# Second attention: the mask goes from a matmul into the running sums on GpSimd, and the query blocks run from last to first

## The chip, the cores and the metric

One Trainium2 chip, one core of it. The metric is the device time of one execution in microseconds (us); lower is better. The kernel before took 2061.19 us in the median of three runs (2055.81, 2061.19 and 2062.60). The profile is of one more execution, which took 2057.08 us.

## The reference, cut to what matters

Two transformer blocks run one after the other on 512 positions of width 1024. The change lies in the attention of the second block ("forgetting attention", 16 heads of 64):

```python
log_f = jax.nn.log_sigmoid(f_logit + b_f)
cum = jnp.cumsum(log_f, axis=1).transpose(0, 2, 1)
for i in range(S // Q_BLOCK):                      # 4 query blocks of 128
    lo, hi = i * Q_BLOCK, (i + 1) * Q_BLOCK
    s = jnp.einsum('bhqd,bhkd->bhqk', q[:, :, lo:hi], k[:, :, :hi]) * scale
    s = s + cum[:, :, lo:hi, None] - cum[:, :, None, :hi]
    s = jnp.where(kpos[None, :] <= qpos[:, None], s, -1e30)
    prob = jax.nn.softmax(s, axis=-1)
    outs.append(jnp.einsum('bhqk,bhkd->bhqd', prob, v[:, :, :hi]))
```

The term `cum[lo:hi]` is constant along a row and drops out of the softmax. Query block i sees 128 x (i + 1) keys, and only its last 128 keys need the mask.

## The kernel before, in words

Each engine has its own program, a list of instructions in a fixed order. Semaphores order them between engines; on an engine nothing overtakes anything. The five programs are `tensor_program` (TensorE, PE), `scalar_program` (ScalarE, ACT), `vector_program` (VectorE, DVE), `pool_program` (GpSimd, POOL) and `sync_program` (SyncE, SP, which issues the weight loads).

Nearly all of the work is dense matmuls of 1024-wide weights. Each product is made of three matmuls of split operands (high times high, low times high, high times low), 24 matmuls of 128 x 512 per weight tile, all on line L719. ACT and DVE split every weight tile into high and low parts (L1259, L1737); SP loads the next tile when a buffer is free.

The second attention runs inside such a stretch. `mix2_order` writes the order out by hand. There are 20 weight tiles (`MIX2`), so 480 dense matmuls. There are 64 score blocks, numbered n. The pair of heads is c = n // 8, the head of the pair is p = n % 2, and the query block is i = n % 8 // 2. Each score block is a step, and step n is followed by a number of slots from the table `share`, by n % 8. The table sums to 32 for each pair of heads. With three more steps at the end this makes 267 slots, and `woven` spreads the 480 dense matmuls evenly over the slots. In step n TensorE issues the transposes of block n - 2 ("turn"), then the scores of block n. In every fourth step (n % 4 == 2) it first issues the value products of blocks n - 5 and n - 3.

A score block goes through the engines in this way:

- TensorE, `fox_scores` (L1128): two matmuls, queries by keys (L918) and queries by the low part of the keys (L921), both 128 x 128(i + 1), into bank 4 or 5. Then a third matmul, identity by `mask_b` in bf16 (L1135), adds 1e30 above the diagonal of the last 128 columns (queries and keys carry the sign so that the smallest score is the largest weight). It first waits until the block two back has been read from that bank (`s_fmin`).
- VectorE, `fox_scores` (L2211): one custom instruction (L2219) adds the row of running sums `at_c` to the scores, writes `at_p`, and takes the row's minimum.
- ScalarE, `fox_scores` (L1609): the exponential with the row sum (L1613).
- VectorE, `fox_divide` (L2222): reciprocal (L2226) and scaling (L2228).
- TensorE, `fox_turn` (L1140): transposes of 128 x 128 (L1146), copied out by ScalarE (L1620). `fox_values` (L1150) multiplies with the values (L1160).

`at_c` has four buffers, one for each head modulo 4, of 128 partitions x 512 sums, all partitions alike. GpSimd loads them from memory (`load_cum`, L2424): heads 0 to 3 at once, head h only when the last block of head h - 4 has been read by L2219. During the stretch these 12 loads are all that GpSimd does.

VectorE and ScalarE also take the dense tiles out of the banks (queries L1930, keys L1942 and L1949, and copies) and split weights. `mix2_scalar_order` and `mix2_vector_order` put these pieces behind the scores and behind the divide of a block, one or two for each block, by the length of the list that is waiting. The queries and keys of pair c + 2 may be written only when the last scores of pair c are listed.

After the stretch come eight gating steps (L1192) among dense matmuls. They need a weight tile `ws`, which GpSimd starts to load when the last value product is done (L2433), and of which VectorE clears a part (L2250).

Of the kernel before, what the change touches and what calls it, by code (L numbers as in the profile page):

```python
# [8 lines left out]
ALU = mybir.AluOpType  # L9
F32 = mybir.dt.float32  # L10
F32R = mybir.dt.float32r
BF16 = mybir.dt.bfloat16

P = 128
# [5 lines left out]
NB = T // P  # L20
# [243 lines left out]
    return out  # L264


def mix2_order():


    share = (5, 3, 3, 3, 4, 4, 5, 5)  # L270
    steps = []
    for n in range(64 + 3):
        s = []
        if n >= 6 and n % 4 == 2:
            s += [("values", n - 5), ("values", n - 3)]
        if 2 <= n < 66:
            s.append(("turn", n - 2))
        if n < 64:
            s.append(("scores", n))
        steps += [s] + [[]] * (share[n % 8] - 1)  # L280
    out, scored, held = [], 0, []
    for what, i in woven(len(MIX2), len(steps), len(MIX2) * 24 / len(steps)):
        if what == "mm":
            out.append((what, i))
        elif what == "end":
            if MIX2[i] < 8 or scored > MIX2[i] % 8 - 2:
                out.append(("evac", i))
            else:
                held.append(i)
            out.append((what, i))  # L290
        else:
            for kind, n in steps[i]:
                out.append((kind, n))
                if kind == "scores" and n % 8 == 7:
                    scored = n // 8 + 1
                    out += [("evac", j) for j in held]
                    held.clear()
    return out
# [66 lines left out]
def block_kernel(nc, io):  # L365
    ctx = ExitStack()
    base = (nc.sbuf_base + 63) // 64 * 64
# [18 lines left out]
    def const(name, shape, dt):  # L386
        nonlocal cat
        n = 2 if dt == BF16 else 4
        for s in shape[1:]:
            n *= s  # L390
        t = sb(name, shape, dt, cat)
        cat += (n + 31) // 32 * 32
        return t
# [5 lines left out]
    gfold = const("gfold_t", [P, ND], F32)  # L399
    ident = const("ident_t", [P, P], F32)  # L400
    ident_b = const("ident_b", [P, P], BF16)
    mask_b = const("mask_b", [P, P], BF16)
    mask1_b = const("mask1_b", [P, P], BF16)
    ones = const("ones_t", [P, 1], F32)
    lnb = const("lnb_t", [P, ND], F32)
# [24 lines left out]
    def ar(name, shape, dt, kb):  # L430
# [32 lines left out]
            for ph, at in (("a", 80), ("b", 44))}  # L463
# [35 lines left out]
    at_pt = [[sb(f"at_pte{p}", [P, 3, P], F32, late + 1536 * p) for p in range(2)],  # L499
             [ar(f"at_pto{p}", [P, 4, P], F32, 76 + 2 * p) for p in range(2)]]  # L500
    at_c = [sb("at_c0", [P, T], F32, late + 3072)] + [ar(f"at_c{i}", [P, T], F32, 78 + 2 * i) for i in (1, 2, 3)]
# [9 lines left out]
    bank = [ctx.enter_context(nc.psum_tensor(f"bank{i}", [P, T], F32)) for i in range(8)]  # L511
# [6 lines left out]
    def signal(name):  # L518
        signals.append(Signal(ctx.enter_context(nc.semaphore(name))))
        return signals[-1]  # L520
# [74 lines left out]
    s_cum = [signal(f"s_cum{i}") for i in range(4)]  # L595
# [25 lines left out]
    s_pair, s_sp_hi, s_sp_lo, s_stick, s_o = signal("s_pair"), signal("s_sp_hi"), signal("s_sp_lo"), signal("s_stick"), signal("s_o")  # L621
    s_o_hi, s_o_lo = signal("s_o_hi"), signal("s_o_lo")
    s_fmin, s_fexp, s_fsum, s_fe, s_ft = signal("s_fmin"), signal("s_fexp"), signal("s_fsum"), signal("s_fe"), signal("s_ft")
    s_f, s_fd, s_cumsum = signal("s_f"), signal("s_fd"), signal("s_cumsum")


# [74 lines left out]
    def tensor_program(e, counting):  # L701
        q = Waits(e, counting)
# [208 lines left out]
        def score(ph, out, c, p, queries, keys, keys_on_rows, start, stop):  # L911
            s = c % 2
            q.wait_ge(s_kl_zero, (ph, s, p))
            q.wait_ge(s_q, (ph, c, 1))
            q.wait_ge(s_k, (ph, c, 1))
            a, k = qs_t[s][p][:, queries], ks_t[s][p][:, keys]
            l, r = (k, a) if keys_on_rows else (a, k)
            e.matmul(out, l, r, start=start, stop=False, skip_group_check=True)  # L918
            k = kl_t[ph][s][p][:, keys]
            l, r = (k, a) if keys_on_rows else (a, k)  # L920
            return e.matmul(out, l, r, start=False, stop=stop, skip_group_check=True)  # L921
# [204 lines left out]
                    lambda i, x=x: [(s_v_dve if i % 2 else s_v_act, ("b", x, i))])  # L1126

        def fox_scores(n):  # L1128
            c, i, p = n // 8, n % 8 // 2, n % 2
            b, w = S_B[p], P * (i + 1)  # L1130
            open_bank(b)
            q.wait_ge(s_ident, 1)
            q.wait_ge(s_mask, 0)
            score("b", bank[b][:, 0:w], c, p, slice(P * i, w), slice(0, w), False, True, False)
            m = e.matmul(bank[b][:, w - P:w], ident_b[:, :], mask_b[:, :], start=False, stop=True,  # L1135
                         skip_group_check=True)
            m.then_inc(*s_out.inc(("fox", n)))
            frees[b] = [(s_fmin, n)]

        def fox_turn(n):  # L1140
            i, p = n % 8 // 2, n % 2
            open_bank(T_B)
            q.wait_ge(s_fe, n)
            q.wait_ge(s_ident, 0)
            for j in range(i + 1):
                m = e.transpose(bank[T_B][:, P * j:P * (j + 1)], at_p[p][:, P * j:P * (j + 1)], ident[:, :])  # L1146
            m.then_inc(*s_out.inc(("turn", n)))
            frees[T_B] = [(s_ft, n)]

        def fox_values(n):  # L1150
            c, i = n // 8, n % 8 // 2
            if i == 0:
                open_bank(O_B)
            for p in range(2):
                q.wait_ge(s_ft, n - 1 + p)
            for j in range(i + 1):
                q.wait_ge(s_v_dve if j % 2 else s_v_act, ("b", c // 4, j))
                for p in range(2):
                    f = P * (c % 4) + 64 * p
                    m = e.matmul(bank[O_B][64 * p:64 * p + 64, P * i:P * (i + 1)], v_b[c // 4][:, j, f:f + 64],  # L1160
                                 at_pt[i % 2][p][:, j, :], start=i == 0 and j == 0, stop=j == i, skip_group_check=True)
            m.then_inc(*s_out.inc(("values", "b", n)))
            if i == NB - 1:
                frees[O_B] = [(s_o, ("b", c))]

        def mix2_freed(name):
# [71 lines left out]
    def scalar_program(e, counting):  # L1238
# [368 lines left out]
            natural([f"nv{x}{k}" for k in range(4)], value_rows(("b", x), v_b[x], ("nv", x)))  # L1607

        def fox_scores(n):  # L1609
            i, p = n % 8 // 2, n % 2  # L1610
            pt, col = at_p[p][:, 0:P * (i + 1)], slice(n % 8, n % 8 + 1)
            q.wait_ge(s_fmin, n)
            e.activation(pt, pt, ACT.Exp, scale=-1.0, bias=mneg[:, col], accum_out=rsum[:, col]).then_inc(*s_fexp.inc(n))  # L1613

        def fox_turn(n):
            i, p = n % 8 // 2, n % 2
            q.wait_ge(s_out, ("turn", n))
            if n >= 4:
                q.wait_ge(s_out, ("values", "b", n - 3 - p))
            e.activation(at_pt[i % 2][p][:, 0:i + 1, :], bank[T_B][:, 0:P * (i + 1)].rearrange("p (j c) -> p j c", c=P),  # L1620
                         ACT.Copy).then_inc(*s_ft.inc(n))
# [96 lines left out]
    def vector_program(e, counting):  # L1718
# [490 lines left out]
            natural([f"nv{x}{k}" for k in range(4)], value_rows(("b", x), v_b[x], ("nv", x)))  # L2209

        def fox_scores(n):  # L2211
            c, i, p = n // 8, n % 8 // 2, n % 2
            h, w = 2 * c + p, P * (i + 1)
            pt, col = at_p[p][:, 0:w], slice(n % 8, n % 8 + 1)
            q.wait_ge(s_out, ("fox", n))
            q.wait_ge(s_cum[h % 4], h)
            if n >= 2:
                q.wait_ge(s_out, ("turn", n - 2))
            e.tensor_tensor_reduce(pt, bank[S_B[p]][:, 0:w], at_c[h % 4][:, 0:w], 1.0, 3e38, ALU.add, ALU.min,  # L2219
                                   mneg[:, col]).then_inc(*s_fmin.inc(n))  # L2220

        def fox_divide(n):  # L2222
            i, p = n % 8 // 2, n % 2
            pt, col = at_p[p][:, 0:P * (i + 1)], slice(n % 8, n % 8 + 1)
            q.wait_ge(s_fexp, n)
            e.reciprocal(rinv[:, col], rsum[:, col]).then_inc(*s_fsum.inc(n))  # L2226
            q.wait_ge(s_fsum, n)
            e.tensor_scalar(pt, pt, rinv[:, col], None, op0=ALU.mult).then_inc(*s_fe.inc(n))  # L2228
# [105 lines left out]
    def pool_program(e, counting):  # L2334
# [20 lines left out]
        def zero_keys(ph, key):  # L2355

            q.wait_ge(s_out, (key, 1))
            for s in range(2):
                for p in range(2):
# [8 lines left out]
                        channel_multiplier=1).then_inc(*s_ident.inc(0))  # L2368
        q.wait_ge(s_ident, 0)
        e.tensor_copy(ident_b[:, :], ident[:, :]).then_inc(*s_ident.inc(1))  # L2370
        e.memset(mask_b[:, :], 0.0).then_inc(*s_mask.inc("zero0"))
        q.wait_ge(s_mask, "zero0")
        e.affine_select(mask_b[:, :], mask_b[:, :], [[-1, P]], ALU.is_ge, 1e30, base=0,
                        channel_multiplier=1).then_inc(*s_mask.inc(0))
        e.memset(mask1_b[:, :], 0.0).then_inc(*s_mask.inc("zero1"))
        q.wait_ge(s_mask, "zero1")
        e.affine_select(mask1_b[:, :], mask1_b[:, :], [[1, P]], ALU.is_gt, -1e30, base=0,
# [46 lines left out]
        def load_cum(h):  # L2424
            q.wait_ge(s_ncs_out, 0)
            if h >= 4:
                q.wait_ge(s_fmin, 8 * ((h - 4) // 2) + 6 + h % 2)
            e.dma_start(at_c[h % 4][:, :], ncs[h:h + 1, :].to_broadcast([P, T])).then_inc(*s_cum[h % 4].inc(h, by=16))

        for h in range(16):  # L2430
            load_cum(h)
        q.wait_ge(s_out, ("values", "b", 63))
        e.dma_start(ws[:, :, :], io["ws"]).then_inc(*s_ws2_in.inc(0, by=16))  # L2433
        q.wait_ge(s_e_out, 0)
# [174 lines left out]
```

## Time and profile before

| what | us |
|---|---|
| median of three runs | 2061.19 |
| lowest, highest | 2055.81, 2062.60 |
| the profiled execution | 2057.08 |
| its span in the profile | 2055.3 |
| PE busy in the span | 2044.5 |
| DVE, ACT, POOL busy in the span | 1084.6, 814.0, 87.4 |

The span runs from the first to the last instruction; the execution's time has 1.8 us more around it. "Busy" of PE is the time in which at least one matmul is under way, by modelled ends; two starts tell more of the pace than a duration does. PE is busy in 99% of the span, so the other engines matter only where they make it wait. The second attention lies between 1227 and 1405 us of the span. TensorE's granted clock is at its full level there.

### The profile page before, as it was taken

The page shows a single profiled execution, that of the slowest core. Times are in us where ns is not written, and L with a number is a line of the kernel's source. Part 1 is how long each engine was busy: PE and PEld are TensorE (multiplying, and loading weights), DVE is VectorE, ACT ScalarE, POOL GpSimd, SP SyncE. Part 2 cuts the span into 40 slices and gives each one's busy share as a digit, 9 for nine tenths or more (in the row PEclk, how much of TensorE's full clock was granted, in tenths as well). Part 3 has the DMA queues.
Part 4 walks back from the last instruction along what each step waited for, and adds up shares of the span by engine and source line. Part 5 has one row for each costly group of instructions (what it writes and reads, how often), then busy time and mean ns, then how long its engine had stood idle before and what let it go on. Part 6 is the DMA issues. An engine that isn't in the chain of part 4 may idle for free.

```text
span 2055.3 us, 25236 instructions
## 1 busy us (share of the span) xinstructions
PE 2044.5 (99%) x10305; PEld 1715.6 (83%) x10305; DVE 1084.6 (53%) x1674; ACT 814.0 (40%) x1274; POOL 87.4 (4%) x122
## 2 busy tenths in 40 slices
PE   9999999999999999999999999999999999999998
PEld 7888888988888898888889787778888988888888
DVE  7645544577743553333335546665425475356546
ACT  6422222456453343222233445554323353234335
POOL 1000000100000010000012000000000100000011
PEclk9999999999999999999999999999999999999999
DMA  9645433443423223232222332222333232333241
GB/s 355 245 139 196 175 104 127 131 159 117 162 74 93 80 83 123 70 122 97 78 85 94 114 123 62 84 82 85 110 92 93 72 103 83 112 103 96 71 151 42
DMA packets 71046, 235.76 MB, mean 115 GB/s; under 512 B 8834, under 2 KB 11138, under 8 KB 70547
## 3 DMA queue, kind: packets, MB, share of 16 engines
q1 hardware_dynamic: 68752, 226.07, 33.1%
q0 software_dynamic: 2032, 7.90, 1.2%
q8 instruction: 82, 1.34, 0.3%
q14 instruction: 34, 0.27, 0.0%
q10 hardware_dynamic: 146, 0.18, 0.0%
HBM read 229.37 MB, written 4.75 MB: 114 GB/s over the span
## 4 chain that ended last, share of the span: by engine, by line
PE 94%; DVE 2%; issue 2%; ACT 1%; POOL 1%; DMA 0%; DVEq 0%; POOLq 0%; ACTq 0%
PE bank L719 83%; PE bank L783 4%; PE bank L1160 1%; PE bank L1146 1%; PE bank L1042 1%; PE bank L918 1%; PE bank L921 1%; POOL ssq L2347 0%; DVE w_lo L1737 0%; PE bank L1072 0%; DVE raw_m L1733 0%; PE bank L944 0%; PE bank L814 0%; PE bank L1192 0%; PE bank L841 0%
## 5 line engine op out<-in xcount | busy, mean ns | idle before, releaser
L1737 DVE TENSOR_TENSOR w_lo<-w_raw,w_hi 128x1024 fp32r<-128x1024 f32 (+2 forms) x345 | 394.9, 1172 | 195.5 <-ACT w_hi L1259 195.0
L719 PE MATMUL bank<-u_hi,w_hi 128*128 128x512 f32 (+1 forms) x1904 | 490.0, 370 | 0.8 <-ACT u_hi L1454 0.8
L719 PE MATMUL bank<-u_hi,w_lo 128*128 128x512 f32 (+1 forms) x1904 | 490.7, 370 | 0.0
L719 PE MATMUL bank<-u_lo,w_hi 128*128 128x512 f32 (+1 forms) x1904 | 489.9, 370 | 0.7 <-DVE u_lo L2007 0.6
L1259 ACT ACTIVATE w_hi<-w_raw 128x1024 fp32r<-128x1024 f32 (+2 forms) x345 | 326.3, 978 | 222.5 <-PE bank L719 169.9
L719 PEld LDWEIGHTS bank<-u_lo,w_hi 128*128 128x128 f32 x1904 | 353.8, 189 | 60.2 <-DVE u_lo L2007 1.4
L719 PEld LDWEIGHTS bank<-u_hi,w_hi 128*128 128x128 f32 x1904 | 353.3, 189 | 59.5 <-ACT u_hi L1454 1.2
L719 PEld LDWEIGHTS bank<-u_hi,w_lo 128*128 128x128 f32 x1904 | 353.4, 189 | 57.4
L1865 DVE TENSOR_TENSOR ff_a<-ff_s,bank 128x512 f32<-128x512 f32 x44 | 30.2, 687 | 223.3 <-issue 207.0
L1335 ACT ACTIVATE act_hi<-ff_a 128x512 fp32r<-128x512 f32 x66 | 41.7, 632 | 262.4 <-DVE ff_a L1865 222.3
L719 PE MATMUL bank<-act_hi,w_lo 128*128 128x512 f32 (+1 forms) x561 | 130.1, 377 | 0.0
L719 PE MATMUL bank<-act_lo,w_hi 128*128 128x512 f32 (+1 forms) x561 | 130.1, 377 | 0.0
L719 PE MATMUL bank<-act_hi,w_hi 128*128 128x512 f32 (+1 forms) x561 | 129.4, 377 | 0.0
L719 PEld LDWEIGHTS bank<-act_hi,w_hi 128*128 128x128 f32 x561 | 101.5, 188 | 19.5
L719 PEld LDWEIGHTS bank<-act_hi,w_lo 128*128 128x128 f32 x561 | 101.5, 188 | 19.3
L719 PEld LDWEIGHTS bank<-act_lo,w_hi 128*128 128x128 f32 x561 | 101.5, 188 | 19.3
L2347 POOL TENSOR_TENSOR ssq<-ssq,sq 128x512 f32<-128x512 f32 (+1 forms) x39 | 49.0, 1255 | 1349.3 <-ACT sq L1287 1348.7
L1891 DVE TENSOR_TENSOR act_lo<-ff_a,act_hi 128x512 fp32r<-128x512 f32 x66 | 45.7, 693 | 51.0 <-ACT act_hi L1335 51.0
L1287 ACT ACTIVATE sq<-hres 128x512 f32<-128x512 f32 (+1 forms) x52 | 28.2, 544 | 110.1 <-DVE hres L1824 65.1
L1880 DVE SCALAR_TENSOR_TENSOR ff_c<-bank,vecs_t,ff_c 128x511 f32<-128x511 f32 (+1 forms) x44 | 33.0, 749 | 60.4 <-ACT ff_c L1349 59.4
L783 PE MATMUL bank<-w_hi,u_hi 128*128 128x512 f32 x160 | 62.3, 389 | 0.0
L783 PE MATMUL bank<-w_lo,u_hi 128*128 128x512 f32 x160 | 62.3, 389 | 0.0
(295 smaller groups left out, 2176.2 us busy)
## 6 DMA issues: line engine op xcount, KB each, us to landing
w_raw<-in_w_gu_dram SPq DMA_DIRECT2D x114, 512.0 KB, 4.2
w_raw<-in_w_ada_dram SPq DMA_DIRECT2D x43, 512.0 KB, 4.6
w_raw<-in_w_mix_dram SPq DMA_DIRECT2D x36, 512.0 KB, 3.6
w_raw<-in_w_dn_dram SPq DMA_DIRECT2D x44, 384.0 KB, 3.1
w_raw<-in_w_dn_dram SPq DMA_DIRECT2D x44, 320.0 KB, 3.3
w_raw<-in_w_in_dram SPq DMA_DIRECT2D x24, 512.0 KB, 3.6
raw_m<-in_w_ada_dram SPq DMA_DIRECT2D x17, 512.0 KB, 12.6
w_raw<-in_w_o_dram SPq DMA_DIRECT2D x16, 512.0 KB, 3.5
```

The source lines that it names most:

```text
L719: m = e.matmul(bank[b][:, c], w, (x.lo if part == 2 else x.hi)[:, k, c], start=start, stop=stop, skip_group_check=True)
L783: m = e.matmul(bank[b][:, :], (x.lo if part == 1 else x.hi)[:, k, P * i:P * (i + 1)], w, start=k == 0 and part == 0, stop=k == 2 * len(til ...
L918: e.matmul(out, l, r, start=start, stop=False, skip_group_check=True)
L921: return e.matmul(out, l, r, start=False, stop=stop, skip_group_check=True)
L1259: e.activation(hi_of(name), raw_of(i), ACT.Copy).then_inc(*s_w_hi.inc(name))
L1287: e.activation((sq, sq2)[x][d % 2][:, c], hres[:, d, c], ACT.Square, **kw).then_inc(*s_sq.inc(*keys))
L1335: e.activation(act_hi[:, i, :], ff_a[m % 3][:, :], ACT.Copy).then_inc(*s_a_hi.inc((tag, h, i)))
L1737: e.tensor_tensor(lo_of(name), raw_of(i), f32(hi_of(name)), ALU.subtract).then_inc(*s_w_lo.inc(name))
L1865: e.tensor_tensor(ff_a[m % 3][:, :], ff_s[m % 3][:, :], psum(f"{tag}u{m}")[:, :], ALU.mult).then_inc(*s_glu.inc((tag, m)))
L1880: e.scalar_tensor_tensor(dst[:, n:T], src[:, 0:T - n], vec("conv_w_2", 44 * k + col), dst[:, n:T], ALU.mult, ALU.add).then_inc(*s_conv.inc ...
L1891: e.tensor_tensor(act_lo[:, i, :], ff_a[m % 3][:, :], f32(act_hi[:, i, :]), ALU.subtract).then_inc(*s_a_lo.inc((tag, h, i)))
L2347: e.tensor_tensor(ssq[x][:, c], ssq[x][:, c], (sq, sq2)[x][d % 2][:, c], ALU.add).then_inc(*s_ssq_pool.inc(*keys))
```

## The change

The mask matmul of each score block is gone, and with it `mask_b`. Instead GpSimd writes 1e30 above the diagonal into the last 128 columns of the row of running sums (`affine_select` on `at_c`, in place, 128 x 128 f32), which VectorE adds to the scores anyway. What is overwritten is not needed again by the head because its query blocks now run from last to first: block 3 (512 keys), then 2, 1 and 0. VectorE's L2219 waits for this select (`s_later`) instead of for the load. The select of block n waits for L2219 of block n - 2, the block of the same head before it, or, for a head's first block, for the load of `at_c`. The loads of the next pair but one now stand in GpSimd's list behind the selects of a pair. The table of slots is turned round with the widths, and the total is now 271 slots. The flags that open and close the bank of the value products follow the new order.

```diff
+def query_block(n):
+    return NB - 1 - n % 8 // 2
 def mix2_order():
-    share = (5, 3, 3, 3, 4, 4, 5, 5)
+    share = (5, 5, 5, 4, 4, 3, 3, 3)
...
-    mask_b = const("mask_b", [P, P], BF16)
...
         def fox_scores(n):                                    # TensorE
-            c, i, p = n // 8, n % 8 // 2, n % 2
+            c, i, p = n // 8, query_block(n), n % 2
             b, w = S_B[p], P * (i + 1)
             open_bank(b)
-            q.wait_ge(s_ident, 1)
-            q.wait_ge(s_mask, 0)
-            score("b", bank[b][:, 0:w], c, p, slice(P * i, w), slice(0, w), False, True, False)
-            m = e.matmul(bank[b][:, w - P:w], ident_b[:, :], mask_b[:, :], start=False, stop=True,
-                         skip_group_check=True)
+            m = score("b", bank[b][:, 0:w], c, p, slice(P * i, w), slice(0, w), False, True, True)
             m.then_inc(*s_out.inc(("fox", n)))
             frees[b] = [(s_fmin, n)]
...
         def fox_values(n):                                    # TensorE
-            c, i = n // 8, n % 8 // 2
-            if i == 0:
+            c, i = n // 8, query_block(n)
+            if i == NB - 1:
                 open_bank(O_B)
...
         def fox_scores(n):                                    # VectorE
...
             q.wait_ge(s_out, ("fox", n))
-            q.wait_ge(s_cum[h % 4], h)
+            q.wait_ge(s_later, n)
...
-        e.memset(mask_b[:, :], 0.0).then_inc(*s_mask.inc("zero0"))      # GpSimd, at the start
-        q.wait_ge(s_mask, "zero0")
-        e.affine_select(mask_b[:, :], mask_b[:, :], [[-1, P]], ALU.is_ge, 1e30, base=0,
-                        channel_multiplier=1).then_inc(*s_mask.inc(0))
...
-        for h in range(16):
+        def hide_later(n):
+            c, i, p = n // 8, query_block(n), n % 2
+            h = 2 * c + p
+            if i == NB - 1:
+                q.wait_ge(s_cum[h % 4], h)
+            else:
+                q.wait_ge(s_fmin, n - 2)
+            y = at_c[h % 4][:, P * i:P * (i + 1)]
+            e.affine_select(y, y, [[-1, P]], ALU.is_ge, 1e30, base=0, channel_multiplier=1).then_inc(*s_later.inc(n))
+        for h in range(4):
             load_cum(h)
+        for n in range(64):
+            hide_later(n)
+            if n % 8 == 7 and n < 48:
+                load_cum(n // 8 * 2 + 4)
+                load_cum(n // 8 * 2 + 5)
```

## Rows read from the trace of the kernel before

**Rows 1.** The page: busy time of PE; the chain that ended last, by engine.

```profile
PE 2044.5 (99%) x10305; PEld 1715.6 (83%) x10305; DVE 1084.6 (53%) x1674; ACT 814.0 (40%) x1274; POOL 87.4 (4%) x122
...
PE 94%; DVE 2%; issue 2%; ACT 1%; POOL 1%; DMA 0%; DVEq 0%; POOLq 0%; ACTq 0%
```

**Rows 2.** Busy us by engine in the attention's stretch; then clock, DMA share, GB/s.

```profile
1227.30:1402.00 174.70, 174.34 (x1114) 137.22 (x1113) 112.70 (x319) 102.05 (x242) 6.56 (x12) 1.00 0.25 76
```

**Rows 3.** Waits of PE from 1227 to 1434: us in total, times, longest.

```profile
PE bank L918 <- DVE ks L1949: 0.3, 1, 0.3
```

**Rows 4.** The mask matmuls, grouped: count | busy us, mean ns | idle before.

```profile
L1135 PE MATMUL bank<-mask_b,ident_b 128*128 128x128 bf16 x64 | 14.7, 230 | 0.0
```

**Rows 5.** PE in order of time, second attention, with mask: start, us, instruction.

```profile
1240.69 0.40 PE L921 MATMUL bank<-klb,qs 128*128 128x512 f32 x1
1240.93 0.23 PE L1135 MATMUL bank<-mask_b,ident_b 128*128 128x128 bf16 x1
1240.97 0.48 PE L719 MATMUL bank<-u_hi,w_lo 128*128 128x512 f32 x1
1241.29 2.01 PE L719 MATMUL bank<-u_lo,w_hi 128*128 128x512 f32 x8
...
1252.92 0.28 PE L921 MATMUL bank<-klb,qs 128*128 128x256 f32 x1
...
1253.09 0.48 PE L719 MATMUL bank<-u_lo,w_hi 128*128 128x512 f32 x1
1253.40 1.31 PE L719 MATMUL bank<-u_hi,w_hi 128*128 128x512 f32 x5
...
1315.27 0.28 PE L921 MATMUL bank<-klb,qs 128*128 128x128 f32 x1
...
1315.43 0.47 PE L719 MATMUL bank<-u_lo,w_hi 128*128 128x512 f32 x1
1315.75 0.63 PE L719 MATMUL bank<-u_hi,w_hi 128*128 128x512 f32 x2
```

**Rows 6.** PE in order of time, first attention's scores, no mask there.

```profile
459.63 0.27 PE L921 MATMUL bank<-qs,kla 128*128 128x128 f32 x1
459.74 0.33 PE L918 MATMUL bank<-qs,ks 128*128 128x256 f32 x1
459.91 0.28 PE L921 MATMUL bank<-qs,kla 128*128 128x256 f32 x1
460.03 0.40 PE L918 MATMUL bank<-qs,ks 128*128 128x512 f32 x1
460.26 0.40 PE L921 MATMUL bank<-qs,kla 128*128 128x512 f32 x1
460.50 1.76 PE L719 MATMUL bank<-u_lo,w_hi 128*128 128x512 f32 x7
462.10 1.75 PE L719 MATMUL bank<-u_hi,w_hi 128*128 128x512 f32 x7
```

**Rows 7.** GpSimd's selects (first attention) and loads: ns min/median/max, start us.

```profile
L2411 POOL TENSOR_SCALAR_AFFINE_SELECT sb_t<-sb_t x32: 292/293/422, 447.8 to 586.4; 128x128 f32<-128x128 f32 x32
...
L2428 POOL DMA_DIRECT2D at_c<-ncs_scratch x16: 546/546/580, 1198.7 to 1354.5; - x16
```

**Rows 8.** One 512-wide block (n = 7) in order of time, to its transposes.

```profile
1244.20 0.69 DVE L2219 CUSTOM_DVE_ANT_0 at_p<-bank,at_c 128x512 f32<-128x512 f32 x1 [0.57 <-PE bank L1135]
...
1245.98 0.49 DVE L2228 TENSOR_SCALAR at_p<-at_p,rinv_t 128x512 f32<-128x512 f32 x1
...
1248.97 0.60 PE L1146 MATMUL bank<-ident_t,at_p 128*128 128x128 f32 x4
```

**Rows 9.** The end of the stretch in order of time: `ws` cleared, first gating.

```profile
1409.39 0.48 DVE L2250 MEMSET ws<- 64x512 f32 x1 [0.16 <-issue]
...
1411.66 1.05 PE L1192 MATMUL bank<-ws,zv 128*128 128x128 f32 x8
```

More of the change, by code:

```diff
@@ L623, in block_kernel @@
     s_fmin, s_fexp, s_fsum, s_fe, s_ft = signal("s_fmin"), signal("s_fexp"), signal("s_fsum"), signal("s_fe"), signal("s_ft")
+    s_later = signal("s_later")
     s_f, s_fd, s_cumsum = signal("s_f"), signal("s_fd"), signal("s_cumsum")
@@ L1140, in fox_turn @@
         def fox_turn(n):
-            i, p = n % 8 // 2, n % 2
+            i, p = query_block(n), n % 2
             open_bank(T_B)
@@ L1160, in fox_values @@
                     m = e.matmul(bank[O_B][64 * p:64 * p + 64, P * i:P * (i + 1)], v_b[c // 4][:, j, f:f + 64],
-                                 at_pt[i % 2][p][:, j, :], start=i == 0 and j == 0, stop=j == i, skip_group_check=True)
+                                 at_pt[i % 2][p][:, j, :], start=i == NB - 1 and j == 0, stop=j == i, skip_group_check=True)
             m.then_inc(*s_out.inc(("values", "b", n)))
-            if i == NB - 1:
+            if i == 0:
                 frees[O_B] = [(s_o, ("b", c))]
@@ L1609, in fox_scores @@
         def fox_scores(n):
-            i, p = n % 8 // 2, n % 2
+            i, p = query_block(n), n % 2
             pt, col = at_p[p][:, 0:P * (i + 1)], slice(n % 8, n % 8 + 1)
@@ L1615, in fox_turn @@
         def fox_turn(n):
-            i, p = n % 8 // 2, n % 2
+            i, p = query_block(n), n % 2
             q.wait_ge(s_out, ("turn", n))
@@ L2211, in fox_scores @@
         def fox_scores(n):
-            c, i, p = n // 8, n % 8 // 2, n % 2
+            c, i, p = n // 8, query_block(n), n % 2
             h, w = 2 * c + p, P * (i + 1)
@@ L2222, in fox_divide @@
         def fox_divide(n):
-            i, p = n % 8 // 2, n % 2
+            i, p = query_block(n), n % 2
             pt, col = at_p[p][:, 0:P * (i + 1)], slice(n % 8, n % 8 + 1)
@@ L2428, in load_cum @@
             e.dma_start(at_c[h % 4][:, :], ncs[h:h + 1, :].to_broadcast([P, T])).then_inc(*s_cum[h % 4].inc(h, by=16))
-        for h in range(16):
-            load_cum(h)
+        def hide_later(n):
+            c, i, p = n // 8, query_block(n), n % 2
+            h = 2 * c + p
[6 more added lines that the diff above has]
+        for h in range(4):
+            load_cum(h)
+        for n in range(64):
[3 more added lines that the diff above has]
+                load_cum(n // 8 * 2 + 5)
         q.wait_ge(s_out, ("values", "b", 63))
```

## The prediction

> **What bounds the kernel now.** I read the page first, for the busy times and the chain that ended last. PE is busy 2044.5 of 2055.3 us, and 94% of the chain is PE [rows 1]. So the question is what TensorE issues, and where it waits. Next I read busy time by stretch: in the second attention, 174.70 us long, PE is busy 174.34 us, at a granted clock of 1.00, the upper of its two levels (2.4 GHz); VectorE is busy 112.70, ScalarE 102.05 and GpSimd 6.56 us [rows 2]. Then the waits of PE: there is one in the stretch, 0.3 us, for a key tile that VectorE was still writing [rows 3]. So the stretch is as long as TensorE's list. A matmul taken from the list gives back its whole place, as long as nothing else becomes late.
>
> **The mask matmuls.** There are 64, shown with a mean of 230 ns [rows 4]. That duration is mostly the pipeline's modelled end, so I don't use it; I go by starts. The pace of 128x512 matmuls is 0.23 us (seven take 1.60 us from 460.50 to 462.10) [rows 6]. I measure from the start of L921, the last true score matmul, to the start of the second dense matmul after it:
>
> - 512 keys, with mask: 1240.69 to 1241.29, 0.60 us [rows 5]. Without one: 460.26 to 460.50 and one pace of 0.23, 0.47 us [rows 6]. Difference 0.13.
> - 256 keys, with mask: 1252.92 to 1253.40, 0.48 [rows 5]. Without: 459.91 to 460.03, and 0.23 from there to L921, 0.35 [rows 6]. Difference 0.13.
> - 128 keys, with mask: 1315.27 to 1315.75, 0.48 [rows 5]. Without: 0.11 from 459.63 to 459.74. The 256-wide matmul that follows there takes 0.17 to its successor, while the next 256-wide one takes 0.12 (459.91 to 460.03). So a 0.05 stall stays behind a 128-wide matmul. That makes 0.11 + 0.05 + 0.23 = 0.39 [rows 6]. Difference 0.09.
> - 384 keys: between its neighbours, 0.12.
>
> So a mask costs little for its own 128 columns (the next matmul starts 0.04 later, 1240.93 to 1240.97) and more by what follows. The dense matmul behind it takes 0.32 instead of 0.23 until its successor starts, since its weights can't be loaded behind so short a matmul. There are 16 blocks of each width: 16 x (0.13 + 0.12 + 0.13 + 0.09) = 7.5 us. Rounding to 0.01 us sixteen times over is worth some tenths, and the 256 and 128 cases are read next to other successors than they will have. I take 7.2 us. The bounds: 64 x 0.04 = 2.6 us if only the mask's own place is saved, and 64 x 0.13 = 8.3 us if the 128-wide blocks gain as much as the others.
>
> The Trainium skill (TensorE: Matmul & The Clock Gate, section "Back-to-back issue gap") gives about 81 ns for each 128-column matmul with its weight load in a steady stream, and about 131 ns for a 512-column one. By its first figure the estimate of the saving would be 64 x 0.081 = 5.2 us. This trace disagrees with the second, with 230 ns for a 512-wide one, and shows 90 to 130 ns for what a mask costs.
>
> **The order of the blocks.** The widths of a head pair are the same set, turned round. Transposes, value products, exponentials and divides keep their counts and sizes: nothing on TensorE. The slots are 271 instead of 267, so a slot holds 1.77 dense matmuls instead of 1.80. These are the same 480 matmuls: nothing. From the scores of a block to its transposes there are now 10, 10, 9, 8, 7, 6, 6 and 8 slots for n % 8 = 0 to 7, where there were 8, 6, 6, 7, 8, 9, 10 and 10. The 512-wide blocks keep ten slots. Such a block is through VectorE 2.27 us after L2219 starts (1244.20 to 1246.47), and its transposes start at 1248.97: 2.5 us to spare [rows 8]. The 128-wide ones keep 6 and 8, the 256-wide 7 and 6 instead of 6 and 7.
>
> I went through the orders that `mix2_vector_order` and its fellows make of the new table. The pieces of VectorE come at nearly the same blocks as before. The one critical place stays: the key copies of pair 4. They were listed behind L2219 and behind the divide of block 31, and the scores of block 32 had to wait 0.3 us for the second [rows 3]. Now both stand one place earlier, the second ahead of the divide of block 31. But blocks 29 to 31 now come only 3 slots apart (about 1.6 us with their own matmuls), and block 29 has two key pieces, so VectorE arrives late. I put the wait at 0.3 us again; between 0 and 1.
>
> **The selects.** These are new: 64 selects of 128x128 on GpSimd. The nearest row is the same operation in the first attention: median 293 ns, up to 422 ns [rows 7]. That is 64 x 0.29 = 19 us of an engine that is busy 6.56 of 174.70 us [rows 2]. A select becomes possible when L2219 of block n - 2 is done, a whole step ahead of need (at least 1.6 us, against 0.3 plus two hand-overs of about 0.1): nothing. It covers itself except at the six changes of head pair where loads stand ahead of it. There the list is: load, load, select of 8c + 8. The second load waits for L2219 of block 8c + 7. It takes 0.55 us [rows 7], the select 0.29, and three hand-overs about 0.3: some 1.1 us after L2219 of 8c + 7 is done. The scores of 8c + 8 follow those of 8c + 7 by three slots (1.2 us) and 0.6 to 0.8 us of transposes and scores, and L2219 of 8c + 7 itself takes 0.3 to 0.5 of it. So the select is in time or a few tenths late. Behind the waiting L2219 stand VectorE's pieces and the divide of block 8c + 8. For them TensorE waits only after ten slots, with those 2.5 us to spare [rows 8]. Cost nothing; from 0 to 6 x 0.5 us if VectorE was late already.
>
> A select may also hold up VectorE or be held up. The Trainium skill (SBUF — State Buffer, section on who reads and writes with whom, the "exclusive lock" of the shared port pair) says that GpSimd and VectorE block each other for a whole instruction when VectorE copies or scales f32 in SBUF. The spread from 293 to 422 ns [rows 7] agrees with that. What it could cost is in the rivals.
>
> Removed at the start: a memset and a select on GpSimd, which nobody waits for: nothing.
>
> **Behind the stretch.** The first gating needs `ws`, cleared by 1409.87, and TensorE is there at 1411.66 [rows 9]: 1.8 us to spare. The load starts at the last value product. Step 66 now has 5 slots behind it instead of 3, so three or four more dense matmuls follow it: 0.8 us more to spare. TensorE's later list is unchanged and moves forward whole.
>
> **Sum.** 7.2 us off; new waits about 0. The profiled execution becomes 2057.1 - 7.2 = 2049.9 us. It lies 4.1 us below the median of 2061.2, within a spread of 7 us over the runs; counted from the median the result is 2054.0 us, which I give.
>
> **Rivals.**
> - A: The mask was nearly free. Only its own place goes, the weight load's stall stays behind the narrower score matmul: 2.6 us, giving 2058.6. For: the spacing behind the mask is 0.04. Against: a 512-wide L921 is followed by dense matmuls at full pace [rows 6]. The skill's 81 ns stand between this and my forecast; what its page would give is said above.
> - B: The saving is there, but VectorE gives part of it back: late in the three-slot steps ahead of each change of pair, or at pair 4's keys. 2 to 4 us back: about 2057. For: those steps are now crowded against the change of pair, where keys are due. Against: VectorE is busy 65% of the stretch.
> - C, the other side: VectorE becomes the bound in blocks 5, 6 and 7 of each pair. If every select holds it up in full, its 112.7 us become 131.4 of some 167. The three steps there give it 4.8 us; at 1.3 to 1.6 us for a block's own instructions, 0.7 to 1.2 for a piece in some, and 0.3 for each hold-up, it is up to 1.5 to 2 us late at the change of pair. There the next scores need a free bank and keys. This decides from 0.9 us of wait for each of the 8 pairs, since then the 7.2 us are used up; at 2 us it is 16 us, giving about 2063. Against: the kernel before has three such short steps in each pair too, and shows a single wait of 0.3.
>
> **How the numbers follow.** Forecast 70%, A 8%, B 15%, C 7%. About 0.3%, or 6.2 us, is what a measurement can tell here from no change. The forecast's 7.2 us is hardly above it, and the runs before spread over 7 us. So of the forecast's 70% I count 56 as faster and 14 as no change; A and B are no change but for 1; C is 6 slower and 1 no change. Faster 0.57, same 0.37, slower 0.06. The range: below, 8.3 us saved from the profiled execution's 2057.1, rounded down: 2048. Above, it takes in A and most of B: 2060. The forecast's own range is 2049 to 2056.
>
> **What would show it.** In the trace after: from L921 to the second dense matmul 0.47 us at 512 keys and 0.39 at 128; the stretch from 1227 to the last value product shorter by 7 us; PE's waits in it below 1 us. Selects of 0.3 to 0.42 us. L2219 released by L921, and by a select at most at n = 8, 16, ..., 48, with nothing on PE behind it. It is wrong if PE shows waits for `at_p` or for L2219 of more than 1 us at each change of pair (C), or if the dense matmul behind L921 still takes 0.32 (A).

## The result, and the profile after

The changed kernel took 2053.24 us in the median of 13 runs (2047.71 to 2054.94); the kernel before, in 13 runs, 2061.20 us (2055.81 to 2062.93). The ratio of the runs is 0.9962, with a 95% interval of 0.9953 to 0.9972. That is 7.8 us faster, between 5.8 and 9.7. The forecast was 2054.0. Runs of either kernel lie mostly in two groups some 5 us apart, and group against group the medians are 2055.97 and 2048.30 us (7.7 less) and 2061.48 and 2053.35 us (8.1 less).

The page of the changed kernel, span and part 1, beside [rows 1]:

```profile
span 2051.5 us, 25281 instructions
...
PE 2041.5 (100%) x10241; PEld 1718.9 (84%) x10241; DVE 1084.5 (53%) x1674; ACT 815.3 (40%) x1274; POOL 111.1 (5%) x184
```

64 matmuls fewer on PE, 64 selects more on POOL less two instructions at the start, and 23.7 us more of POOL's time. DVE's busy time is the same to 0.1 us. The span alone is only 3.8 us shorter than before; the other 4 us are covered by a lower granted clock in this one execution, told of in the last section. So I compare the attention's stretch.

Busy us by engine from the first score matmul to the end of the last value product, first the kernel before, then the changed one ([rows 2] had a slightly shorter window):

```profile
1227.08:1404.73 177.65, 177.29 (x1148) 139.50 (x1146) 112.72 (x319) 104.19 (x245) 6.56 (x12) 1.00 0.25 75
1231.35:1400.19 168.84, 168.84 (x1081) 137.61 (x1079) 112.73 (x319) 105.47 (x245) 30.01 (x74) 1.00 0.26 79
```

67 matmuls fewer are in it, the 64 masks and three dense ones that the new table puts behind it. PE of the changed kernel is busy in every moment, and no wait of PE is listed from 1227 to 1434 us. The 0.3 us for a key tile in [rows 3] is gone. From the first score matmul to the first gating matmul, between which both kernels have the same work but for the masks, it was 184.58 us (1227.08 to 1411.66) and is 176.46 us (1231.35 to 1407.82): 8.1 us shorter.

PE of the changed kernel in order of time, two 512-wide blocks at a change of head pair, beside [rows 5]:

```profile
1250.70 0.27 PE L1147 MATMUL bank<-ident_t,at_p 128*128 128x128 f32 x1
1250.73 0.48 PE L923 MATMUL bank<-ks,qs 128*128 128x512 f32 x1
1251.05 0.39 PE L926 MATMUL bank<-klb,qs 128*128 128x512 f32 x1
1251.28 2.00 PE L724 MATMUL bank<-u_hi,w_lo 128*128 128x512 f32 x8
1253.11 0.39 PE L724 MATMUL bank<-u_lo,w_hi 128*128 128x512 f32 x1
1253.35 0.27 PE L1147 MATMUL bank<-ident_t,at_p 128*128 128x128 f32 x1
```

(L926 is the old L921, L724 the old L719.) Behind L926 the dense matmuls run at once at their pace: 1251.28 to 1253.11 are eight of 0.229 us. Before, the first of them took 0.32. The weight loads show why (PEld, first the kernel before, then the changed one):

```profile
1240.93 0.20 PEld L719 LDWEIGHTS bank<-u_hi,w_lo 128*128 128x128 f32 x1
1241.06 0.65 PEld L719 LDWEIGHTS bank<-u_lo,w_hi 128*128 128x128 f32 x3
```

```profile
1251.05 0.88 PEld L724 LDWEIGHTS bank<-u_hi,w_lo 128*128 128x128 f32 x4
```

Before, the weights of the second dense matmul began to load at 1241.06, when the first had been running since 1240.97; it started 0.23 us later, at 1241.29. The median over the blocks is a load 0.083 us late in every width. In the changed kernel it begins 0.003 us after the first dense matmul has started (0.051 at 128 keys), and again the second starts 0.23 to 0.24 us after its load.

GpSimd of the changed kernel at the same place:

```profile
1248.68 0.57 POOL L2425 DMA_DIRECT2D at_c<-ncs_scratch  x1 [2.48 <-DVE mneg_t L2220]
1250.31 0.54 POOL L2425 DMA_DIRECT2D at_c<-ncs_scratch  x1 [1.06 <-DVE mneg_t L2220]
1250.85 0.60 POOL L2436 TENSOR_SCALAR_AFFINE_SELECT at_c<-at_c 128x128 f32<-128x128 f32 x2
```

and VectorE, which needs the first of these two selects for block 8, and then block 9, whose select was long done:

```profile
1249.92 0.08 DVE L2220 DVE_READ_ACCUMULATOR2_ANT mneg_t<- 128x1 f32 x1
...
1251.48 0.69 DVE L2220 CUSTOM_DVE_ANT_0 at_p<-bank,at_c 128x512 f32<-128x512 f32 x1 [0.43 <-POOL at_c L2436]
...
1254.11 0.69 DVE L2220 CUSTOM_DVE_ANT_0 at_p<-bank,at_c 128x512 f32<-128x512 f32 x1 [0.20 <-PE bank L926]
```

From VectorE's end of block 7 (1250.00) to the select's end (1251.20) are 1.2 us. VectorE starts block 8 at 1251.48, 0.43 us behind the start of L926 (1251.05). That is the same distance as at block 9 (1253.69 to 1254.11), where it waited for the scores alone. So at block 8 too the scores came last, although the view puts the 0.43 us down to the select. It names a select twice in the whole stretch (blocks 8 and 32), 0.9 us together:

```profile
L2436 POOL TENSOR_SCALAR_AFFINE_SELECT at_c<-at_c x64: 282/293/1145, 1210.1 to 1389.2; 128x128 f32<-128x128 f32 x64
...
  DVE at_p L2220: 0.9, 2
```

### The profile page after: what moved, and what is told of

The parts are those of the page before. It is cut to its first block, busy times and chain, and to the rows that moved or that the text cites. A ratio compares the mean times of both kernels' runs of the same rounds, so it can differ in the third digit from the quotient of the medians.

```text
span 2051.5 us, 25281 instructions
## 1 busy us (share of the span) xinstructions
PE 2041.5 (100%) x10241; PEld 1718.9 (84%) x10241; DVE 1084.5 (53%) x1674; ACT 815.3 (40%) x1274; POOL 111.1 (5%) x184
## 4 chain that ended last, share of the span: by engine, by line
PE 94%; DVE 2%; issue 2%; ACT 1%; POOL 1%; DMA 0%; DVEq 0%; POOLq 0%; ACTq 0%
PE bank L724 83%; PE bank L788 4%; PE bank L1147 1%; PE bank L1161 1%; PE bank L1047 1%; PE bank L923 1%; PE bank L926 1%; POOL ssq L2348 0%; DVE w_lo L1738 0%; PE bank L1077 0%; DVE raw_m L1734 0%; DMA w_raw<-in_w_mix_dram 0%; PE bank L949 0%; PE bank L819 0%; PE bank L1193 0%
## 5 line engine op out<-in xcount | busy, mean ns | idle before, releaser
L724 PE MATMUL bank<-u_hi,w_hi 128*128 128x512 f32 (+1 forms) x1904 | 489.3, 369 | 0.4 <-ACT u_hi L1455 0.4
L724 PE MATMUL bank<-u_lo,w_hi 128*128 128x512 f32 (+1 forms) x1904 | 488.2, 369 | 0.8 <-DVE u_lo L2008 0.7
L724 PE MATMUL bank<-u_hi,w_lo 128*128 128x512 f32 (+1 forms) x1904 | 488.1, 368 | 0.0
L724 PEld LDWEIGHTS bank<-u_lo,w_hi 128*128 128x128 f32 x1904 | 353.8, 189 | 60.1 <-DVE u_lo L2008 1.4
L724 PEld LDWEIGHTS bank<-u_hi,w_hi 128*128 128x128 f32 x1904 | 353.6, 189 | 59.6 <-ACT u_hi L1455 0.8
L724 PEld LDWEIGHTS bank<-u_hi,w_lo 128*128 128x128 f32 x1904 | 354.1, 189 | 58.4 <-issue 0.2
L724 PE MATMUL bank<-act_lo,w_hi 128*128 128x512 f32 (+1 forms) x561 | 131.0, 379 | 0.0
L724 PE MATMUL bank<-act_hi,w_lo 128*128 128x512 f32 (+1 forms) x561 | 130.5, 378 | 0.0
L724 PE MATMUL bank<-act_hi,w_hi 128*128 128x512 f32 (+1 forms) x561 | 129.4, 376 | 0.0
L724 PEld LDWEIGHTS bank<-act_lo,w_hi 128*128 128x128 f32 x561 | 102.4, 190 | 19.3
L724 PEld LDWEIGHTS bank<-act_hi,w_lo 128*128 128x128 f32 x561 | 101.7, 189 | 19.3
L724 PEld LDWEIGHTS bank<-act_hi,w_hi 128*128 128x128 f32 x561 | 101.5, 188 | 19.5
```

What stands on the lines that cost most here:

```text
L724: m = e.matmul(bank[b][:, c], w, (x.lo if part == 2 else x.hi)[:, k, c], start=start, stop=stop, skip_group_check=True)
```

## The experiments

My theory: the gain is the place of the mask matmuls on PE (7 to 7.5 us) and the one wait at block 32 (0.6 us from where the scores should have started); the selects and the new order cost and bring nothing else. Rivals: the order and the table bring a good part of it; the selects cost something that the saving hides. The times in the second column are from one trace each, from the first score matmul of the second attention to its first gating matmul; the ratios are of 4 to 13 runs of a kernel against 13 to 29 of the kernel before.

| kernel | us from first score to first gating | ratio to before, 95% interval |
|---|---|---|
| before | 184.58 | 1 |
| changed | 176.46 | 0.9962 (0.9953 to 0.9972) |
| order and table alone | 183.92 | 0.9997 (0.9987 to 1.0007) |
| mask left out, old order | 178.05 | 0.9966 (0.9952 to 0.9979) |
| changed, mask matmul kept | 183.95 | 0.9991 (0.9982 to 1.0001) |
| before, mask matmul twice | 188.04 | 1.0020 (1.0010 to 1.0030) |
| before, mask matmul first | 183.86 | 0.9992 (0.9982 to 1.0003) |
| changed, old table | 177.90 | 0.9964 (0.9951 to 0.9977) |
| changed, selects 4 times | 176.47 | 0.9958 (0.9943 to 0.9972) |
| changed, selects 8 times | 245.18 | 1.0287 (1.0271 to 1.0302) |

### The order alone

```diff
-    share = (5, 3, 3, 3, 4, 4, 5, 5)
+    share = (5, 5, 5, 4, 4, 3, 3, 3)
...
-            c, i, p = n // 8, n % 8 // 2, n % 2
+            c, i, p = n // 8, query_block(n), n % 2
```

(the kernel before, with `query_block` in all programs, and the flags of the value bank with it)

> The kernel before with the query blocks from last to first and the table of slots turned round, the mask matmuls kept and nothing new on GpSimd. Theory (the 7.5 us are the mask matmuls' place, 0.6 us is the one wait of PE at block 32, which the new order removes): 0.6 us faster than before, about 0.03%, not to be told from no change in the time; in the trace no wait of PE from the first score block to the first gating. Rival (the order and the table bring a good part of the gain, by making VectorE less late): 3 us faster or more.

Measured: 0.66 us shorter in the trace, ratio 0.9997. No wait of PE is listed in the stretch. The theory holds; a gain of 3 us (ratio 0.9985) lies below the interval. The one wait of the kernel before, at block 32 (PE in order of time), was longer than its row had said:

```profile
1311.38 0.60 PE L1146 MATMUL bank<-ident_t,at_p 128*128 128x128 f32 x4
1312.32 0.30 PE L918 MATMUL bank<-ks,qs 128*128 128x128 f32 x1 [0.34 <-DVE ks L1949]
```

The last of the four transposes started at 1311.71, and the scores 0.61 us later, where 0.03 is usual.

### The mask left out

```diff
-            score("b", bank[b][:, 0:w], c, p, slice(P * i, w), slice(0, w), False, True, False)
-            m = e.matmul(bank[b][:, w - P:w], ident_b[:, :], mask_b[:, :], start=False, stop=True,
-                         skip_group_check=True)
+            m = score("b", bank[b][:, 0:w], c, p, slice(P * i, w), slice(0, w), False, True, True)
```

> The kernel before with the mask matmuls left out and nothing in their place (so the mask of the second attention is not applied), in the old order. Theory: 7 to 7.5 us faster than before, ratio 0.9965; in the trace the time from L921 to the second dense matmul is 0.47 us at 512 keys and 0.40 at 128, where it was 0.60 and 0.48; the wait at block 32 stays, 0.5 us. Rival (order brings it): 5 us or less.

Measured: ratio 0.9966 (7 us), 6.5 us shorter in the trace. Take the starts from the second score matmul of a block to the last dense matmul of its run, for all 64 blocks, and add the runs of dense matmuls from there to the first gating. The sum is 119.30 us in the kernel before, 111.85 us here and 111.79 us in the changed kernel. So the place of the masks is 7.5 us, 0.117 us each: 2.8 of it up to the start of the first dense matmul, 4.7 between the first and the second. Part of it went into waits, because PE now reached them sooner (PE's waits, 1220 to 1434 us):

```profile
PE bank L918 <- DVE ks L1947: 0.6, 1, 0.6
PE bank L1144 <- DVE at_p L2226: 0.2, 1, 0.2
```

The two rows are 0.5 us more than the 0.3 of [rows 3]; another 0.4 us is lost between value products, which the list does not name. That is a part I had not seen: with the mask gone, the old order gives back 1 us in new waits. With the masks the new order is worth 0.66 us, without them 178.05 - 176.46 = 1.6 us.

### The mask matmul kept beside the selects

```diff
-            m = score("b", bank[b][:, 0:w], c, p, slice(P * i, w), slice(0, w), False, True, True)
+            q.wait_ge(s_ident, 1)
+            q.wait_ge(s_mask, 0)
+            score("b", bank[b][:, 0:w], c, p, slice(P * i, w), slice(0, w), False, True, False)
+            m = e.matmul(bank[b][:, w - P:w], ident_b[:, :], mask_b[:, :], start=False, stop=True,
+                         skip_group_check=True)
...
```

(and `mask_b` again, with its memset and select at the start)

> The changed kernel with the mask matmuls kept as well, so the mask is applied twice (by TensorE and by GpSimd's selects). Theory (the selects and the waits for them cost nothing): the same time as the kernel with the order alone, 0.6 us faster than before, 7.5 us slower than the changed kernel. Rival (the selects hold VectorE up and cost something that the saving hides): 1 us or more slower than the kernel with the order alone.

Measured: 183.95 us, against 183.92 with the order alone and no selects. So the selects, their waits and the loads behind them cost nothing that two traces can tell (0.03 us). 183.95 - 176.46 = 7.5 us is the mask's place once more.

### The mask matmul twice

```diff
-            m = e.matmul(bank[b][:, w - P:w], ident_b[:, :], mask_b[:, :], start=False, stop=True,
-                         skip_group_check=True)
+            for _ in range(2):
+                m = e.matmul(bank[b][:, w - P:w], ident_b[:, :], mask_b[:, :], start=False, stop=True,
+                             skip_group_check=True)
```

> The kernel before with each mask matmul issued twice in a row (the mask is added twice). Theory (a mask costs its own place of some 0.06 us, and the f32 weight load that can't hide behind it costs the rest, once for a run of short matmuls): the second one adds only 64 x 0.06 = 3.8 us, ratio 1.0018. Rival (each mask costs its 0.117 us by itself): 7.5 us, ratio 1.0036. By the 81 ns that the Trainium skill gives for a 128-column matmul (TensorE: Matmul & The Clock Gate, section Back-to-back issue gap) the estimate would be 5.2 us.

PE of this kernel in order of time, one 512-wide block:

```profile
1240.29 0.40 PE L921 MATMUL bank<-klb,qs 128*128 128x512 f32 x1
1240.53 0.29 PE L1136 MATMUL bank<-mask_b,ident_b 128*128 128x128 bf16 x2
1240.62 0.47 PE L719 MATMUL bank<-u_hi,w_lo 128*128 128x512 f32 x1
1240.93 2.00 PE L719 MATMUL bank<-u_lo,w_hi 128*128 128x512 f32 x8
```

From L921 to the second dense matmul it is 0.64 us here, 0.60 with one mask [rows 5]; in the median of the 512-wide blocks 0.649 and 0.592. All in all 3.46 us more in the trace, 0.054 each, and a ratio of 1.0020 (4 us). The second mask costs half of the first: the dense matmul behind the pair still takes 0.31 us (1240.62 to 1240.93), once. The number is the theory's; its reason, that a run of short matmuls pays once, fails in the next experiment.

### The mask matmul first

```diff
-            score("b", bank[b][:, 0:w], c, p, slice(P * i, w), slice(0, w), False, True, False)
-            m = e.matmul(bank[b][:, w - P:w], ident_b[:, :], mask_b[:, :], start=False, stop=True,
-                         skip_group_check=True)
+            e.matmul(bank[b][:, w - P:w], ident_b[:, :], mask_b[:, :], start=True, stop=False, skip_group_check=True)
+            m = score("b", bank[b][:, 0:w], c, p, slice(P * i, w), slice(0, w), False, False, True)
```

> The kernel before, old order, the mask matmul issued as the first of a block's three matmuls instead of the last, so it stands behind the transposes, where the next f32 weight load is exposed anyway, and L921 stands before the dense matmuls. Theory: only its own place of about 0.06 us is left for 62 of 64 blocks, 64 x 0.117 - 64 x 0.06 = 3.7 us faster than before. Rival (a mask costs the same wherever it stands): no change.

Measured: 0.7 us shorter in the trace, ratio 0.9992 (1.6 us, interval -0.6 to 3.7). The expected 3.7 us did not come. PE in order of time, first this kernel, then the kernel before:

```profile
1247.08 0.49 PE L1145 MATMUL bank<-ident_t,at_p 128*128 128x128 f32 x3
1247.41 0.22 PE L1134 MATMUL bank<-mask_b,ident_b 128*128 128x128 bf16 x1
1247.44 0.48 PE L918 MATMUL bank<-ks,qs 128*128 128x512 f32 x1
1247.75 0.40 PE L921 MATMUL bank<-klb,qs 128*128 128x512 f32 x1
1247.99 1.99 PE L719 MATMUL bank<-u_hi,w_hi 128*128 128x512 f32 x8
```

```profile
1240.07 0.55 PE L1146 MATMUL bank<-ident_t,at_p 128*128 128x128 f32 x3
1240.38 0.48 PE L918 MATMUL bank<-ks,qs 128*128 128x512 f32 x1
```

Behind L921 the dense matmuls now have their full pace, which gives back the 7.5 us. In front, the three transposes take 0.33 us until the mask starts, 0.11 each, the last like the others; then come 0.03 us to L918, and L918 takes 0.31 until L921, where 0.23 is its pace. In the kernel before, L918 stands behind the last transpose by the same 0.03 us (1240.35 to 1240.38) and takes the same 0.31 (to 1240.69). So that stall was there already, and the mask adds one more step of 0.11 us: 6.8 us over the blocks. I had reasoned that a run of short matmuls pays once. It pays at each of them: a transpose or a mask takes 0.11 to 0.12 us, whether f32 or bf16 weights come next. The value products, with 64 columns of weights and two heads in turn, take less, 0.055 us on the average, and so does the second mask behind a mask.

### The old table of slots

```diff
-    share = (5, 5, 5, 4, 4, 3, 3, 3)
+    share = (5, 3, 3, 3, 4, 4, 5, 5)
```

> The changed kernel with the old table of slots (5, 3, 3, 3, 4, 4, 5, 5), so that the 512-wide blocks come first and have only 8 and 6 slots to their transposes, and the 128-wide 10 and 10. Theory: a 512-wide block needs 2.8 us from L926 to the end of its scaling, and six slots with their own matmuls are about 3.4 us; with a weight split in between it is late by some tenths: 0 to 2 us slower than the changed kernel, with waits of PE at the transposes of block 1, 9, 17 and so on. Rival (turning the table round was not needed): no wait, same time. Other rival (it was the heart of the change): 5 us slower or more.

Measured: 177.90 us, 1.4 us longer than the changed kernel, as the theory had it in size; the ratio 0.9964 can't be told from 0.9962. But the time is not lost at block 1 of every pair. Two waits of PE are listed, 0.7 and 0.2 us, at the transposes of blocks 0 and 1; by starts, 0.3 us more went at block 43 and under 0.1 at 19 and 35. The longest (PE in order of time):

```profile
1229.09 1.52 PE L724 MATMUL bank<-u_hi,w_lo 128*128 128x512 f32 x6
1231.28 0.63 PE L1147 MATMUL bank<-ident_t,at_p 128*128 128x128 f32 x4 [0.66 <-DVE at_p L2229]
```

Turning the table round is worth having and is not the heart of the change.

### Selects four and eight times

```diff
...
+            for r in range(3):                     # 7 in the other kernel
+                e.affine_select(y, y, [[-1, P]], ALU.is_ge, 1e30, base=0, channel_multiplier=1).then_inc(*s_again.inc((n, r)))
+                q.wait_ge(s_again, (n, r))
             e.affine_select(y, y, [[-1, P]], ALU.is_ge, 1e30, base=0, channel_multiplier=1).then_inc(*s_later.inc(n))
```

> The changed kernel with each select of GpSimd done four times, one after the other, before VectorE is told. Theory (a select costs nobody anything as long as GpSimd is done before the scores come): 4 x 0.35 = 1.4 us for each step, the shortest step is 1.6 us: 0 to 1 us slower than the changed kernel, with small waits of VectorE and none of PE. Rival (a select holds VectorE up in full while it runs): 192 more of them are 56 us more for VectorE, which is busy 113 of 169 us, so VectorE is at its limit and PE waits 5 us or more in all.

> The changed kernel with each select done eight times. Theory: 8 x 0.35 = 2.8 us for each block on GpSimd, against 2.6 us of a mean step and 1.6 of the shortest: GpSimd becomes the bound of the stretch, 64 x 2.8 = 179 us and more against 169, and PE waits: 10 to 25 us slower than the changed kernel. Rival (VectorE held up in full by 448 more selects, 131 us more on its 113): 70 us slower or more.

Four times: 176.47 us, the same as once, so 192 selects more are free for PE. Here VectorE does wait for selects, six times and 7.1 us in all, and starts 0.14 us after a select's end; PE waits for nothing. Eight times: 68.7 us longer, between the theory's 10 to 25 and the rival's 70 or more. Which of them is right the rows must tell. GpSimd of the kernel with eight, in order of time:

```profile
1266.30 2.90 POOL L2437 TENSOR_SCALAR_AFFINE_SELECT at_c<-at_c 128x128 f32<-128x128 f32 x7
1269.34 0.29 POOL L2439 TENSOR_SCALAR_AFFINE_SELECT at_c<-at_c 128x128 f32<-128x128 f32 x1
...
1276.24 3.96 POOL L2437 TENSOR_SCALAR_AFFINE_SELECT at_c<-at_c 128x128 f32<-128x128 f32 x7
1280.34 0.29 POOL L2439 TENSOR_SCALAR_AFFINE_SELECT at_c<-at_c 128x128 f32<-128x128 f32 x1
```

and busy us by engine in its stretch, in the order PE, PEld, DVE, ACT, POOL:

```profile
1231.00:1476.00 245.00, 191.54 (x1121) 143.55 (x1121) 117.64 (x320) 106.73 (x254) 165.70 (x507) 0.99 0.19 62
```

Eight selects take 3.3 us (1266.30 to 1269.59), 0.41 each with the wait between them, not the 0.35 that I had; and a good microsecond more where VectorE splits a weight meanwhile (1276.24 to 1280.34 against the usual 3.04). From the first select that waits for VectorE (1229.46) to the end of the last one (1458.44) GpSimd is never idle for longer than 0.3 us: 229 us for the selects of 62 blocks and the loads between them. GpSimd is the bound, and the mechanism was right. The price of the theory was 18% too low, and it left the splits and the loads out, so its 10 to 25 us were far off. The rival's number is close, but its reason is gone: VectorE is busy 117.6 us in this stretch, 4.9 more than with one select, where being held up in full by 448 more selects would have made 131 more. One more split is 1.2 us of the 4.9, and about 1.6 are instructions that grew longer.

## Why the prediction was right

- **What bounds it.** PE's list. In the changed kernel PE is busy for 168.84 of 168.84 us.
- **The mask matmuls.** The rows gave 7.5 us and I took 7.2; the sum over all blocks is 7.5. By width, from the start of the second score matmul to that of the second dense one after it, the medians of the changed kernel are 0.465, 0.404, 0.350 and 0.405 us for 512, 384, 256 and 128 keys; foreseen 0.47, (0.41), 0.35 and 0.39. The first attention's matmuls, which have no mask behind them, were a good stand-in [rows 6]. Rival A (2.6 us) fails at L926, behind which the dense matmuls have their pace from 256 keys on; behind a 128-wide L926 a stall of some 0.05 us stays, as foreseen.
- **The 81 ns for a 128-column matmul** of the Trainium skill (TensorE: Matmul & The Clock Gate, section "Back-to-back issue gap"). The traces disagree on both sides: the first mask costs 0.117 us, the second in a row 0.054. One figure can't hold both. What makes the second cheaper, that its weights are those of the first or that bf16 follows bf16, was not tried.
- **The order.** I said nothing, and left the wait at pair 4 at 0.3 us. It went. The row of waits had told only half of it: the transposes ahead of block 32 took 0.61 us until the scores began, where 0.03 is usual. So 0.58 us were lost there, and all of it came back. VectorE's lateness in the three-slot steps, which I feared in rivals B and C, did not show. With the masks kept this is nearly the whole gain of the order (0.66 us). With the masks gone the same order spares one more microsecond.
- **The selects.** Foreseen 0.29 us each and nothing on PE; measured median 0.293, and 0.03 us on PE, which two single traces can't tell from nothing. At the change of pair I put the select 1.1 us behind VectorE's last block, in time or a few tenths late; it was 1.2 us and in time, 0.28 us ahead of VectorE's start. I had their longest wrong: up to 1.145 us instead of 0.42.
- **The sum.** 7.2 foreseen, 8.1 in the trace: 7.5 from the masks and 0.6 from the wait. In the ratio 7.8. Both terms were put too low, by 0.3 and 0.6 us, and nothing made up for it.
- **Rival C.** Its price was added up wrongly: 16 us more on 2054.0 are 2070 us, not 2063. The point from which it decides (0.9 us of wait in each pair) was not neared: even with four selects for one PE lost nothing.

## What to carry to other kernels

Price a short matmul by starts, from the matmul ahead of it to the second one behind it, not by its duration and not by its own columns: here 128 columns of bf16 cost 0.117 us, of which 0.07 was a stall behind the next matmul, whose successor's weights were loaded late. What is added before a reduction anyway (here a row of sums) can carry a mask, if an idle engine can write it a step ahead and the order of the blocks lets it be overwritten. When work is taken from the bounding engine, look at the waits that it will now reach sooner: the same cut was worth 6.5 us in the old order and 7.5 in the new one.

## What the runs showed of the hardware

GpSimd's select is held while VectorE splits a weight. VectorE and GpSimd of the changed kernel in order of time:

```profile
1244.82 1.22 DVE L1738 TENSOR_TENSOR w_lo<-w_raw,w_hi 128x1024 fp32r<-128x1024 f32 x1
```

```profile
1245.05 1.14 POOL L2436 TENSOR_SCALAR_AFFINE_SELECT at_c<-at_c 128x128 f32<-128x128 f32 x1 [1.90 <-DVE mneg_t L2220]
```

The select started 0.23 us into the split and took 1.14 us instead of 0.29, until 0.15 us after the split's end. The split took 1.22 us, as it does alone. All selects of this kernel that took over 0.31 us in the attention end at this distance, 0.15 us, behind a split, a scaling or a cast of VectorE. The Trainium skill (SBUF — State Buffer, section "SBUF: two separate sides", on the exclusive lock of the shared port pair) says that a VectorE instruction with two inputs in SBUF and a GpSimd one that reads SBUF block each other for a whole instruction, whichever starts first. The trace agrees for this direction. In the other VectorE is held for less than a select's 0.29 us: with eight selects, splits that started 0.06 and 0.11 us behind a select took 1.31 and 1.26 us, with four one that started 0.18 behind took 1.23. That agrees with a lock that a select gives back some 0.14 us after its start (an estimate from these splits). Scalings of 384 columns took 0.51 us instead of 0.42 beside the eightfold selects. The eight selects of 0.42 us in the first attention, which the prediction took for a sign of this, each stood beside a TENSOR_TENSOR with both inputs in SBUF, not beside a copy or a scaling.

A bf16 weight load behind a transpose did not hide any better than an f32 one: 0.11 us (median 0.109) from the last transpose to the mask in the kernel with the mask first, and 0.109 from transpose to transpose.

TensorE's granted clock at the start differs between executions. The first 20 us, in the trace of before and then of after (the clock is the column before the last two):

```profile
0.00:20.00 20.00, 18.57 (x89) 16.09 (x90) 10.36 (x23) 14.09 (x19) 1.87 (x11) 0.83 0.93 357
```

```profile
0.00:20.00 20.00, 18.57 (x77) 16.31 (x78) 9.12 (x21) 11.37 (x16) 1.43 (x9) 0.76 0.92 357
```

From 20 to 45 us it was 1.00 before and 0.92 after. By 45 us the changed kernel's execution was 3.3 us behind, and it lost a further 1 us between 1061 and 1138 us, at 0.98. It is why the two spans differ by 3.8 us only, while the attention's stretch differs by 8.1. Of the ten traces two more have 0.74 and 0.75 in the first 20 us (the mask first, the order alone), and the other six have 0.91. What makes an execution start on the lower level (1.2 GHz) for longer was not tried.
